# One kernel of two model blocks on one core: splits of weights further ahead, a longer attention pipeline, the retention's mean taken out of its values, and a start with two partial sums

## The reference

```python
def rmsnorm(x, w):
    y = xf * lax.rsqrt(jnp.mean(xf * xf, axis=-1, keepdims=True) + NORM_EPS)
    return (y * w.astype(jnp.float32)).astype(x.dtype)

def head_groupnorm(o, w, b):
    mu = jnp.mean(of, axis=-1, keepdims=True)
    var = jnp.mean(jnp.square(of - mu), axis=-1, keepdims=True)
    y = ((of - mu) * lax.rsqrt(var + GN_EPS)).reshape(B, S, H * dv)
    return y * w.astype(jnp.float32) + b.astype(jnp.float32)

# retention, 4 heads of 128 (q, k) and 256 (v), written here without its chunks:
#   o[i] = sum over j <= i of (q[i] . k[j]) * decay[h, i - j] * v[j];  then head_groupnorm(o) * silu(rg)
# window attention, 16 heads of 64: softmax over 128 keys with a sink, then @ v
# first attention, 16 heads of 64: p = softmax(q @ k - slope * distance), scaled by a gate, then @ v
```

## Time and profile before

| | us |
|---|---|
| three runs | 1892.69, 1890.19, 1890.25 (median 1890.25) |
| the profiled execution | 1888.81 |
| its span, first to last instruction | 1886.6 |
| PE busy | 1801.2 |
| DVE busy | 972.9 |
| ACT busy | 861.6 |
| POOL busy | 170.0 |

### The profile page before, as it was taken

One profiled execution on the slowest core, in us unless ns is written; L12 is line 12 of the kernel. 1 busy time (PEld: TensorE's weight loads), 2 busy tenths in 40 slices (PEclk: granted clock), 3 DMA queues, 4 the chain that ended last, 5 costly groups with the idle time before them and its releaser, 6 DMA issues.

```text
span 1886.6 us, 24538 instructions
## 1 busy us (share of the span) xinstructions
PE 1801.2 (95%) x9970; PEld 1458.5 (77%) x9970; DVE 972.9 (52%) x1680; ACT 861.6 (46%) x1461; POOL 170.0 (9%) x293
## 2 busy tenths in 40 slices
PE   6899998899999999998999999999899999999997
PEld 4677786679988877875877777877688878888886
DVE  7878555854854464244345545355454543443323
ACT  6445666645463344235346554266543552322223
POOL 2000227510000000000000000022200001111000
PEclk9899999999999999999999999999999999999999
DMA  4563431035423223211322223211123313332332
GB/s 137 168 197 115 135 107 55 1 109 200 147 104 101 89 91 122 90 46 45 109 86 72 78 70 99 93 58 66 57 90 100 101 62 95 91 105 93 93 102 64
DMA packets 61471, 181.30 MB, mean 96 GB/s; under 512 B 7136, under 2 KB 20256, under 8 KB 58928
## 3 DMA queue, kind: packets, MB, share of 16 engines
q1 hardware_dynamic: 61360, 179.75, 29.9%
HBM read 165.57 MB, written 16.25 MB: 96 GB/s over the span
## 4 chain that ended last, share of the span: by engine, by line
PE 75%; DVE 12%; ACT 9%; POOL 3%; issue 2%; DMA 0%; SPq 0%; DVEq 0%; ACTq 0%
PE bank L990 17%; PE bank L991 17%; PE bank L992 17%; PE bank L1084 2%; PE bank L1086 2%; DVE wlo L2103 2%; PE bank L1085 2%; POOL Ps L2881 2%; PE bank L1247 2%; ACT L1521 1%; PE bank L1226 1%; ACT whi L1516 1%; ACT Ps L2000 1%; PE bank L1010 1%; PE bank L1011 1%
## 5 line engine op out<-in xcount | busy, mean ns | idle before, releaser
L2103 DVE TENSOR_TENSOR wlo<-wraw,whi 128x1024 fp32r<-128x1024 f32 (+1 forms) x262 | 316.5, 1210 | 333.0 <-ACT whi L1516 331.9
L990 PE MATMUL bank<-Hh,whi 128*128 128x512 f32 (+2 forms) x1104 | 444.5, 403 | 12.2 <-DVE wlo L2103 12.0
L992 PE MATMUL bank<-Hh,wlo 128*128 128x512 f32 (+2 forms) x1104 | 432.9, 392 | 0.0
L991 PE MATMUL bank<-Hl,whi 128*128 128x512 f32 (+2 forms) x1104 | 432.6, 392 | 0.0
L1516 ACT ACTIVATE whi<-wraw 128x1024 fp32r<-128x1024 f32 (+1 forms) x262 | 271.9, 1041 | 293.1 <-PE bank L992 225.7
L990 PEld LDWEIGHTS bank<-Hh,whi 128*128 128x128 f32 (+2 forms) x1104 | 207.5, 188 | 69.7 <-DVE wlo L2103 14.1
L992 PEld LDWEIGHTS bank<-Hh,wlo 128*128 128x128 f32 (+2 forms) x1104 | 207.4, 188 | 46.0
L991 PEld LDWEIGHTS bank<-Hl,whi 128*128 128x128 f32 (+2 forms) x1104 | 207.7, 188 | 45.3 <-issue 2.2
L1521 ACT ACT_TABLE_LOAD x101 | 129.6, 1283 | 2.9 <-DVE epst L2128 1.1
L2874 POOL TENSOR_SCALAR bs<-dist 128x256 f32<-128x256 f32 x16 | 7.3, 456 | 808.7 <-DMA dist<-in_c_dist 807.9
L990 PE MATMUL bank<-Bh,whi 128*128 128x512 f32 x192 | 76.5, 399 | 0.0
(11 more groups left out here) (394 smaller groups left out, 3240.3 us busy)
## 6 DMA issues: line engine op xcount, KB each, us to landing
wraw<-in_w_o SPq DMA_DIRECT2D x24, 512.0 KB, 3.5
wraw<-in_w_bgate SPq DMA_DIRECT2D x24, 512.0 KB, 3.4
wraw<-in_w_branch SPq DMA_DIRECT2D x24, 512.0 KB, 3.5
wraw<-in_w_fg SPq DMA_DIRECT2D x22, 512.0 KB, 3.5
wraw<-in_w_fu SPq DMA_DIRECT2D x22, 512.0 KB, 3.4
wraw<-in_w_glu SPq DMA_DIRECT2D x16, 512.0 KB, 3.4
wraw<-in_w_fd SPq DMA_DIRECT2D x16, 512.0 KB, 3.5
scratch_CA<-CA SPq DMA_DIRECT2D x4, 1152.0 KB, 6.6
```

The source lines that it names most:

```text
L990: pe.matmul(o, wh[:, cols], hi(k), start=k == 0, stop=False)
L991: pe.matmul(o, wh[:, cols], lo(k), start=False, stop=False)
L992: m = pe.matmul(o, wl[:, cols], hi(k), start=False, stop=k == K - 1)
L2103: dve.tensor_tensor(c.wlo[q][:, 0:n], c.raw[i % RR][:, 0:n], c.whi[q][:, 0:n].bitcast(F32), S_).then_inc(*up(DID, ("wlo", i)))
```

## The change

It has five parts.

1. `with_weights`: `low` reaches to `i + LOOK + 1` at every new piece, and `pump` one piece further while `late` holds.
2. Start: the squares go into two sums (`nacc` and `sq[1]`), which `total_x` adds with two products into one bank; ACT loads the log table right after the squares (`tables`); the second piece's split by ACT comes after `inv`.
3. First attention: the transposes run one unit later, the products with v at odd steps, the last step of a `t` is its own stage; P lies in 16 overlapping places of one space (`P_AT`), and a unit waits for the last earlier one that shared its space, at least 5 units back.
4. Retention: each head's mean is taken out of `rv` when `rv` is evicted (ACT copies 256 wide with a sum, DVE subtracts sum/256), so `ret_mean` is gone; the squares are taken from the banks ahead of `ret_o`, and `head_inv` moves up one unit.
5. Window attention: `wb(i - 1)` stands ahead of `wa(i)`, and POOL's bias is a step of its own (`wbias`), one unit ahead.

The diff, cut to its core (lists of step names, memory of `rvs`, and the places where `P_before` and `summed` are called are left out):

```diff
@@ -303,8 +303,8 @@
                 for i in uses[s[0]](s):
                     if i > seen:
                         seen = i
-                        low(i + 1)
-                        pump(i + LOOK)
+                        low(i + LOOK + 1)
+                        pump(i + LOOK + late)
                         low(i)
                         if not late:
                             low(i + LOOK)
@@ -328,11 +328,16 @@
         self.tick()
         for k in range(KT):
             self.step("x", k)
-            self.square("x", k, 0, k == 0)
-        self.step("pump", 1)
+            self.square("x", k, k // 4, k % 4 == 0)
+        self.step("tables")
+        self.step("pump", 0)
         self.step("consts")
         self.step("nsa_in")
-        self.inv("x", 0, 7, 0, 1.0 / D, "rs")
+        self.bank.take(("total", "x"))
+        self.step("total_x")
+        self.step("inv", "x", 0, 1.0 / D, "rs")
+        self.bank.give(("total", "x"))
+        self.step("pump", 1)
         self.tick()
         self.step("vecs")
         for k in range(KT + 1):
@@ -478,22 +483,28 @@
         def stage_d(u):
             t, a, j = units[u]
             self.step("nd", u)
+
+        def stage_e(u):
+            t, a, j = units[u]
             if j == 3:
+                self.step("no", u)
                 self.bank.give(("o", t))
                 self.step("split_g0", t)
         n = len(units)
-        for i in range(n + 6):
+        for i in range(n + 7):
             if i < n:
                 stage_a(i)
             if i % 3 != 2:
                 self.tick()
             if i % 2 == 0 and 2 <= i <= n:
                 self.step("nb", i - 2)
-            if 3 <= i <= n + 2:
-                stage_c(i - 3)
-            if i % 2 == 0 and i >= 6:
-                stage_d(i - 6)
-            if i == AWAY + 4:
+            if 4 <= i <= n + 3:
+                stage_c(i - 4)
+            if i % 2 and i >= 7:
+                stage_d(i - 7)
+            if i % 2 == 0 and i >= 8:
+                stage_e(i - 8)
+            if i == AWAY + 5:
                 self.step("x_again")
@@ -788,14 +799,10 @@
         units = [(h, kt) for h in range(4) for kt in range(4)]
         def ending(h):
+            self.head_squares(("r", h))
             self.step("ret_o", h)
             for e in range(2):
                 self.bank.give(("ro", h, e))
-            yield
-            self.bank.take(("rm", h))
-            self.step("ret_mean", h)
-            self.bank.give(("rm", h))
-            self.head_squares(("r", h))
             yield
             self.head_inv(("r", h), 1, "hr")
             for e in range(2):
@@ -821,9 +828,8 @@
                     next(post)
         self.drain()
         self.gemm("w_ga", 0, "h2", M=16)
-        next(post)
+        next(post, None)
         self.gemm("w_g", 0, "h2")
-        next(post, None)
         self.gemm("w_g", 4, "h2")
         self.step("fence", 3)
@@ -902,11 +908,15 @@
                         self.bank.take(("ws", u, jj))
                         self.bank.give(("ws", u, jj))
                 self.step("ws", i)
+            if 1 <= i <= n:
+                self.step("wb", i - 1)
+            if i == 0:
+                self.step("wbias", 0)
+            if i < n - 1:
+                self.step("wbias", i + 1)
             if i < n:
                 self.step("wa", i)
             self.tick()
-            if 1 <= i <= n:
-                self.step("wb", i - 1)
@@ -1119,6 +1129,13 @@
         pe.matmul(bank(("total", gen)), c.ones[:, :], c.nacc[acc][:, :], start=True, stop=True).then_inc(
             *up(PE, ("total", gen)))
+    def total_x():
+        on.wait_ge(*at("ones"))
+        for half in range(2):
+            on.wait_ge(*at("acc", "x", 4 * half + 3))
+            m = pe.matmul(bank(("total", "x")), c.ones[:, :], c.summed("x", half), start=half == 0, stop=half == 1)
+        m.then_inc(*up(PE, ("total", "x")))
+
@@ -1369,14 +1386,6 @@
                           start=(kt == 0), stop=(kt == 3))
         x.then_inc(*up(PE, ("rp", u)))
-    def ret_mean(h):
-        b = bank(("rm", h))
-        on.wait_ge(*before(plan.bank, ("rm", h)))
-        on.wait_ge(*at("ro", h))
-        for e in range(2):
-            x = pe.matmul(b, c.ones[:, :], c.ro[h % 2][:, e, :], start=(e == 0), stop=(e == 1))
-        x.then_inc(*up(PE, ("rm", h)))
-
@@ -1861,9 +1873,19 @@
         table("exp_and_others")
         act.activation(s, s, ACT.Exp, scale=-0.5).then_inc(*up(DID, ("rst_e",)))
+    def ev_rv(key):
+        _, m, t = key
+        on.wait_ge(*at("tile", key))
+        on.wait_ge(*at("rsTc"))
+        for g in range(2):
+            h = 2 * m + g
+            x = copy(c.rv[:, t, h * 256:h * 256 + 256], bank(key)[:, g * 256:g * 256 + 256], scale=c.rsT[:, t:t + 1],
+                     accum_out=c.rvs[:, t, h:h + 1])
+        x.then_inc(*up(DID, ("freed", key), ("rvraw", m, t)))
+
     def ev_rows(key):
         name, m, t = key
-        dst = {"w_rv": c.rv, "w_gv": c.gv}[name]
+        dst = c.gv
         on.wait_ge(*at("tile", key))
         on.wait_ge(*at("rsTc"))
         x = copy(dst[:, t, m * 512:m * 512 + 512], bank(key), scale=c.rsT[:, t:t + 1])
@@ -1889,9 +1911,8 @@
         for e in range(2):
             key = ("hq", gen, e)
             on.wait_ge(*before(plan.sqb, key))
-            if e == 0:
-                on.wait_ge(*at("rc", h))
-            x = act.activation(c.sqb[plan.sqb.of[key]], c.head_in[kind](h, e), ACT.Square)
+            on.wait_ge(*at("rp", 4 * h + 3))
+            x = act.activation(c.sqb[plan.sqb.of[key]], bank(("ro", h, e)), ACT.Square)
         x.then_inc(*up(DID, ("hsq", gen)))
     def head_inv(gen, eps, dst):
@@ -2546,12 +2567,13 @@
         dve.tensor_tensor(c.sT[u % 3][:, 0:W], bank(("rs", u))[:, 0:W], c.dec[:, h, 0:W], M).then_inc(
             *up(DID, ("sT", u), ("freed", ("rs", u))))
-    def ret_mean(h):
-        o, b = c.ro[h % 2], bank(("rm", h))
-        on.wait_ge(*at("rm", h))
-        for e in range(2):
-            x = dve.scalar_tensor_tensor(o[:, e, :], b, -1.0 / 256, o[:, e, :], M, A_)
-        x.then_inc(*up(DID, ("rc", h), ("freed", ("rm", h))))
+    def ev_rv(key):
+
+        _, m, t = key
+        v = c.rv[:, t, m * 512:m * 512 + 512].rearrange("p (g d) -> p g d", g=2)
+        total = c.rvs[:, t, 2 * m:2 * m + 2].unsqueeze(2).broadcast_to([128, 2, 256])
+        on.wait_ge(*at("rvraw", m, t))
+        dve.scalar_tensor_tensor(v, total, -1.0 / 256, v, M, A_).then_inc(*up(DID, *([("w_rv",)] if (m, t) == (1, 3) else [])))
@@ ...
     def P(self, u):
-        return (self.Pb if u < AWAY else self.Pl)[u % 4]
+        return (self.Pb if u < AWAY else self.Pl)[u // 8 % 2, u % 8]
+    P_AT = (14, 15, 8, 0, 2, 5, 12, 8)
+    def P_span(self, u):
+        kb = u % 8 // 2 + 1
+        at = self.P_AT[u % 8]
+        return (at, at + kb) if u // 8 % 2 == 0 else (16 - at - kb, 16 - at)
+    def places(self, name, at):
+        place = {}
+        for n in range(16):
+            lo, hi = self.P_span(n)
+            place[n // 8, n % 8] = self.nc.alloc_sbuf_tensor_at(
+                f"{name}{n}", [128, 2, (hi - lo) * 128], F32, offset=at + lo * 1024)[:, :, :]
+        return place
+    def P_before(self, u):
+        lo, hi = self.P_span(u)
+        for v in range(u - 1, -1 if u < AWAY else AWAY - 1, -1):
+            vlo, vhi = self.P_span(v)
+            if vlo < hi and lo < vhi:
+                assert u - v >= 5
+                return v
+        return None
+    def summed(self, gen, acc):
+        return self.sq[1] if (gen, acc) == ("x", 1) else self.nacc[acc][:, :]

```

More of the change, by code:

```diff
@@ L1592, in early, with tables @@
         on.wait_ge(*at("epst"))
+    def tables():
+        table("natural_log")
     def vecs():
@@ L2209, in na @@
         on.wait_ge(*at("bias", t, a))
-        if u >= 4:
-            on.wait_ge(*at("p", u - 4, len(plan.nsa_parts(plan.units[u - 4][2])) - 1))
-            on.wait_ge(*at("pn", u - 4, 0))
-            on.wait_ge(*at("pn", u - 4, 1))
+        v = c.P_before(u)
+        if v is not None:
+            on.wait_ge(*at("p", v, len(plan.nsa_parts(plan.units[v][2])) - 1))
+            on.wait_ge(*at("pn", v, 0))
+            on.wait_ge(*at("pn", v, 1))
         elif u == 0:
@@ L2941, in x_again @@
     def x_again():
-        for u in range(AWAY - 4, AWAY):
+        for u in range(AWAY - 5, AWAY):
             on.wait_ge(*at("p", u, len(plan.nsa_parts(plan.units[u][2])) - 1))
@@ L3141, in first_mixer @@
         self.Rh = h.take("Rh", [128, 4, 2, 8, 64])
-        self.Pl = [h.take(f"Pl{i}", [128, 2, 512])[:, :, :] for i in range(4)]
+        self.Pl = self.places("Pl", h.at)
         x = Region(self.nc, self.X_at)
@@ L3146, in first_mixer @@
         self.tB = [x.take(f"tB{i}", [128, 8, 16]) for i in range(2)]
-        x = Region(self.nc, self.X_at)
-        self.Pb = [x.take(f"Pb{i}", [128, 2, 512])[:, :, :] for i in range(4)]
+        self.Pb = self.places("Pb", self.X_at)
```

(1 more changed line is left out.)

37 lines of the change are left out of this document (18 added, 19 removed).

## The result

The changed kernel takes 1869.32 us (median of 4, 1866.44 to 1870.51); the kernel before, beside it, 1890.86. The ratio is 0.9882 (95% interval 0.9865 to 0.9899): 1.2% faster, where I forecast 1849 and, over all cases, 1836 to 1866. Its profiled span is 1868.7, against 1886.6 before: 17.9 us, where my sum gives 41. The profiled execution of the changed kernel is its slowest of the four (1870.51) and that of the kernel before (1888.81) is faster than all four of its own (1890.19 to 1892.69); by the medians 21.5 us were gained.

The account below looks back on a forecast made before the run. PE, busy 1801.2 of 1886.6 us, was taken as the bound. Terms +3.5 - 8 - 10.5 - 16 - 10 = -41 us took 1888.8 to 1847.8, plus 1.4 for the median: 1849 us, range 1840 to 1857, over all cases 1836 to 1866.

Parts of the forecast that it names:

- splits: First projections: three PE waits for wlo shrink by 3.9 us and three clock falls go (5.1); -8 us, range -3 to -10.
- first attention: Transposes one unit later take away two thirds of 16.5 us of PE waits and clock loss; -10.5 us, range -3 to -16.5.
- retention: Two products per head (6.8 us), waits for ro (5.7) and two clock falls (3.4) go; -16 us, range -12 to -16.5.
- start: whi_55, wlo_58 and constants delay the first norm; +3.5 us (3 to 4), or about 2 us by the skill page's drain.
- window attention: Maxima no longer wait for POOL's scaling, so PE's waits for ss and Ps go; -10 us, range -4 to -13.
- ACT's half moves up as well, so it is not what ends last: First projections: three wlo waits shrink by DVE's prep rows, 3.9 us, to 1.4, 0.6 and 1.0 us.
- by that alone all would go: First attention: one unit's more time, about 2.8 us, for each P exceeds the longest wait, 2.4; 16.5 us at most.
- Rival 1: DVE and POOL become the bound in both attentions, which give only 3 and 4 us; 1863 us, chance 0.23.
- a wait of 2 us or more costs about 1.7 us extra: PE anywhere: after such a wait the clock is partly low, costing about 1.7 us on top of the wait.
- `head_inv` moves into their place, but its input, the squares, is now read from the banks ahead of `ro` and needs no mean: Retention: head_inv takes the place of the removed products and its input is ready without the mean; within the -16 us.
- The slower rival (P's space): First attention: scores wait for older transposes sharing P's space; at 0.7 us per unit, 1905 us, chance 0.03.
- The signs: PE's first product at 22.7 to 23.8, wlo waits at most 1.4, none for ro, first attention 5 to 7, ss near zero.

Follow-up runs that it names:

- b_pump: The changed kernel with the reach of the weight splits in the first projections put back as before (pump to i + LOOK also while late); 1864.68 us, ratio 0.9861.
- m_low: The changed kernel with start reordered, split reach put back, one unit between head_inv and ret_out, and DVE's low parts of four weight pieces early again; 1848.64 us.
- q_late: m_low with DVE's low part of a finished group in the first attention (zsr) a step of its own, one unit later; 1841.27 us, ratio 0.9737.
- d_ret: The changed kernel with one more unit between the retention's head_inv and ret_out; 1864.10 us, ratio 0.9861.

## Why the forecast was wrong

**The sum's error** is 23 us: splits 9.7, first attention 6.0, clock between 509 and 744 us 4.4, retention 4.1, start 0.5, and -1.5 for the window attention. The forecast of "faster" was right, the size half of it.

**Splits: the step that failed** is "ACT's half moves up as well, so it is not what ends last", and "since the piece's raw load or ACT can end last by a little". I had looked at what the split waits for on DVE and not at what its transfer waits for, nor at what stands behind it on ACT. The load is issued at 78.55 (77.85 in b_pump, whose products are 0.7 us earlier there), wherever the split stands; ahead of the copies, the split holds them for 12.5 us. The price was 4.7 us more on one wait, and the term of -8 came out as +1.7. m_low shows that the DVE half of the edit gives what I had summed (7.7); beside it, b_pump and the changed kernel show that the ACT half took it back. That the load can end last "by a little" was right for m_low (0.63 us).

**First attention.** The step that failed is "by that alone all would go" with two thirds as a discount. Of 15.4 us of waits 13.5 are left, and the part came out at -4.5. Rival 1 (DVE and POOL become the bound), with 3 us for this part, was nearer in size; its reason was only in part right. One unit's time more for P moved PE's waits from POOL's P (10.2 to 3.2) to what comes behind it: the copy of the transposes on ACT, which stands behind exp, which stands behind maxima on DVE, which stand behind `zsr`, where DVE waits for ACT. Taking that one wait away (q_late) gave 3.9 of waits, most of it at the maxima (3.7) and little at the copy (1.5), with 1.3 back at P; taking 13.6 us of other DVE rows away gave 2.2. What the remaining 8 us wait for is not settled.

**The clock.** The step that failed is "a wait of 2 us or more costs about 1.7 us extra". 11.9 of the 41 us (7 falls) were summed with it. The first trace speaks against it already: behind PE's start it has eleven waits of 2 us or more, and four of them (ending at 292.1, 349.7, 370.4 and 1360.8) have no fall of the clock, while two falls (near 318 and 1250) follow shorter waits, the longest of them 1.51 and 1.82. The second trace of the same kernel has the same waits and other falls, so a wait makes a fall possible and does not bring it. The changed kernel's trace has two stretches between 509 and 744 us that the first trace lacks, 3.4 us long near 687 and 6.8 near 734, and is 4.4 us longer there, a little under half of their length. Nor do the prices of a wait and a fall always add up: in the window attention the 1.6 us that the fall near 1250 cost came back at the next wait. The Trainium skill (TensorE: Matmul & The Clock Gate, Part 1) says that what grants the clock runs free of the kernel's start. The two traces of the kernel before, with falls at other products, agree, and I had not weighed it. A fall should have been priced by its share over several traces, or left to the range.

**Retention.** The removed work (6.8), waits (5.7) and falls were as summed: with the one new wait gone, d_ret's part is 16.7 us shorter where the sum had 16. The step that failed is "`head_inv` moves into their place, but its input, the squares, is now read from the banks ahead of `ro` and needs no mean": I followed its input and not its result. `hr` needs two table loads on ACT (874.10 and 876.10), DVE stands at the scaling until 878.06, and the six rows of `ret_out` stand ahead of the next `sT`: 2.9 us of wait and a fall of 1.7, as d_ret shows. The mean's new work was hidden, as forecast: from 740 to 800 PE is busy all 60 us in both traces.

**Start and window attention** came near what was worked out: the chain of `whi_55`, `wlo_58` and the constants (+4.0 for +3.5), and a cycle without POOL's scaling (-11.5 for -10). At the start two errors met: `rs` ends at 16.60 and not by 15.8, because ACT waits for PE's second product of the sum (it starts at 11.86, behind the last add, and takes 2.07; "costs nothing, since PE is idle there" left that out), and the chain behind it is 0.5 shorter. The Trainium skill (ScalarE: Activation LUTs, "What ACT_TABLE_LOAD costs") has a drain behind a table load, by which the prediction estimated a start that costs about 2 us. Here the load at 14.68 ends at 15.96 and `rs` follows at 15.97, so the trace shows none. The slower rival (P's space) showed in no wait.

**The signs** that I had named told it: PE's waits in the first attention are 13.5 us and not 5 to 7, the waits for `wlo` reach 6.68 and not 1.4, and `hr` is waited for, by DVE (2.72) and through it by PE. PE's first product (23.69), the wait for `ro` (gone) and those for `ss` (0.2) came as named.

## What to carry to other kernels

Before a step is moved ahead in an in-order list, read when its own input is issued and what will stand behind it if that is late: the same edit gave -8 us with DVE's half alone and +1.7 with ACT's half beside it. A stage's waits are not a sum that one more step of distance gives back; find the chain that ends last next. And price a stretch of low clock over several traces, since one trace's stretches belong to that execution, and only where no wait behind it can take it up.
